# Expert biases of a mixture-of-experts kernel: gate's and up's selection products on two halves of TensorE's rows

## The reference

```python
counts = jnp.bincount(e_flat, length=N_EXPERTS)
padded = (counts + MOE_BLOCK - 1) // MOE_BLOCK * MOE_BLOCK
...
def expert_block(args):
    xb, e = args
    gu = xb @ w_gate_up[e] + b_gate_up[e]
    gate, up = jnp.split(gu, 2, axis=-1)
    gate = jnp.minimum(gate, SWIGLU_LIMIT)
    up = jnp.clip(up, -SWIGLU_LIMIT, SWIGLU_LIMIT)
    act = (up + 1.0) * gate * jax.nn.sigmoid(SWIGLU_ALPHA * gate)
    return act @ w_down[e] + b_down[e]
```

## Time and profile before

| | us |
|---|---|
| median of 3 runs | 2225.14 |
| lowest and highest | 2224.36, 2225.99 |
| profiled execution, its time | 2224.99 |
| its span in the trace | 2222.9 |
| TensorE busy | 2153.6 (97%) |
| VectorE busy | 1488.8 (67%) |
| ScalarE busy | 1075.6 (48%) |
| expert loop | some 1140, from 307 to about 1447 |

### The profile page before, as it was taken

The page is one execution under the profiler, slowest core; times in us unless marked ns, Lnnn a source line. Parts: engine busy times, 40 slices in busy tenths (PEclk is TensorE's granted clock), DMA queues, the critical chain, the costliest instruction groups (busy, mean ns, idle before and its releaser), DMA issues.

```text
span 2222.9 us, 26223 instructions
## 1 busy us (share of the span) xinstructions
PE 2153.6 (97%) x8888; PEld 1436.8 (65%) x8888; DVE 1488.8 (67%) x1474; ACT 1075.6 (48%) x1006; POOL 236.5 (11%) x239
## 2 busy tenths in 40 slices
PE   8999999999999999999999999959999999999998
PEld 3445447777777777777777777624654557888886
DVE  3953459999999999999999999843642323333333
ACT  1010147777777777777777777620003423222222
POOL 0003301211111121111112111100000000000000
PEclk9998989999999999999999999969999999999999
DMA  6123379999999999999999999822131011222220
GB/s 259 57 83 118 120 290 344 379 373 385 368 387 371 384 377 375 379 375 383 373 384 376 377 379 373 325 68 76 48 105 38 38 38 68 99 104 99 100 90 38
DMA packets 77757, 522.38 MB, mean 235 GB/s; under 512 B 10208, under 2 KB 10736, under 8 KB 21392
## 3 DMA queue, kind: packets, MB, share of 16 engines
q1 hardware_dynamic: 65088, 483.68, 56.0%
q0 software_dynamic: 9168, 31.01, 5.5%
q10 hardware_dynamic: 3456, 7.06, 1.0%
HBM read 500.72 MB, written 18.99 MB: 234 GB/s over the span
## 4 chain that ended last, share of the span: by engine, by line
PE 92%; DVE 5%; ACT 1%; DMA 1%; issue 0%; SPq 0%; DVEq 0%; ACTq 0%; POOLq 0%
PE bank L1021 21%; PE bank L1023 21%; PE bank L1022 21%; PE bank L887 8%; PE bank L1133 6%; DVE room L1338 3%; PE bank L1176 3%; PE bank L1234 2%; PE bank L1037 1%; PE bank L1148 1%; PE bank L993 1%; PE bank L1029 1%; PE bank L1206 1%; PE bank L1225 1%; PE bank L896 1%; PE bank L1188 1%
## 5 line engine op out<-in xcount | busy, mean ns | idle before, releaser
L1485 DVE TENSOR_TENSOR ring_r<-ring,room_r 128x2048 fp32r<-128x2048 f32 x384 | 873.5, 2289 | 89.6 <-ACT room_r L637 86.7
L637 ACT ACTIVATE room_r<-ring 128x2048 fp32r<-128x2048 f32 x384 | 735.5, 1916 | 189.1 <-PE bank L1023 183.4
L1021 PE MATMUL bank<-room_r 128*96 128x512 f32 x1536 | 606.7, 395 | 3.5 <-DVE room_r L1517 1.9
L1023 PE MATMUL bank<-room_r 128*96 128x512 f32 x1536 | 602.7, 392 | 0.0
L1022 PE MATMUL bank<-ring_r,room_r 128*96 128x512 f32 x1536 | 602.5, 392 | 0.0
L1021 PEld LDWEIGHTS bank<-room_r 128*96 128x96 f32 x1536 | 248.4, 162 | 105.9 <-DVE ring_r L1485 4.4
L1023 PEld LDWEIGHTS bank<-room_r 128*96 128x96 f32 x1536 | 248.2, 162 | 106.2
L1022 PEld LDWEIGHTS bank<-ring_r,room_r 128*96 128x96 f32 x1536 | 248.5, 162 | 101.4
L1133 PE MATMUL bank<-room,ring 128*128 128x512 f32 x320 | 140.4, 596 | 0.0
L1021 PE MATMUL bank<-room_r,ring_r 128*128 128x512 f32 x352 | 137.0, 389 | 0.9 <-DVE room_r L1736 0.9
L1023 PE MATMUL bank<-room_r,ring_r 128*128 128x512 f32 x352 | 136.9, 389 | 0.0
(11 more groups left out here) (249 smaller groups left out, 2189.5 us busy)
## 6 DMA issues: line engine op xcount, KB each, us to landing
ring<-in_wmoe SPq DMA_DIRECT2D x384, 1024.0 KB, 11.7
ring<-in_wf SPq DMA_DIRECT2D x33, 1024.0 KB, 4.8
ring<-in_wp SPq DMA_DIRECT2D x9, 2048.0 KB, 7.8
ring<-in_wd SPq DMA_DIRECT2D x7, 2048.0 KB, 8.6
ring<-in_wd SPq DMA_DIRECT2D x3, 1024.0 KB, 8.3
room<-in_xT SPq DMA_DIRECT2D x2, 1024.0 KB, 8.6
room<-in_xtok ACTq DMA_DIRECT2D x1, 2048.0 KB, 7.7
h_rows<-room POOLq DMA_DIRECT2D x4, 512.0 KB, 3.0
```

The source lines that it names most:

```text
L637: act.activation(w_hi[s_ % PAIRS], raw_w[ORDER[s_]], ACT.Copy)\
L1021: pe.matmul(out, x_hi, w_hi, start=start, stop=False, skip_group_check=True)
L1023: return pe.matmul(out, x_lo, w_hi, start=False, stop=stop, skip_group_check=True)
L1485: dve.tensor_tensor(w_lo[i], raw_w[i], w_hi[s_ % PAIRS].bitcast(F32), ALU.subtract)\
```

## The change

The host repeats the table four times over the partitions, so that 0 to 63 and 64 to 127 both carry it, and `expert` is p mod 32 everywhere. The addition of 1 covers all partitions; the subtraction is made twice, for partitions 32 to 63 and 96 to 127, and both waits for `bias_split` ask for 2. `biases` makes gate's product with rows 0 to 63 of the array and up's with rows 64 to 127. The order of the instructions on each engine stays; VectorE gets one more ahead of the loop.

```diff
             pool.wait_ge(s["bias_in"], 16)
-            up_bias = braw.rearrange("p (c h n) -> p c h n", c=CHUNKS, h=2)[0:2 * E, :, 1, :]
+            up_bias = braw.rearrange("p (c h n) -> p c h n", c=CHUNKS, h=2)[:, :, 1, :]
             pool.tensor_scalar(up_bias, up_bias, 1.0, None, ALU.add).then_inc(s["bias_one"], 1)
...
                 elif s_ == 0:
-                    act.wait_ge(s["bias_split"], 1)
+                    act.wait_ge(s["bias_split"], 2)
...
-            pe.wait_ge(s["bias_split"], 1)
+            pe.wait_ge(s["bias_split"], 2)
...
                 for h in range(2):
                     q = 2 * c + h
-                    pe.matmul(bank[q][0:CAP, :], sel_cur, bias_tab[:, q * 512:(q + 1) * 512], start=True, stop=False,
-                              skip_group_check=True)
+                    rows = slice(2 * E * h, 2 * E * (h + 1))
+                    pe.matmul(bank[q][0:CAP, :], sel_cur[rows, :], bias_tab[rows, q * 512:(q + 1) * 512], start=True,
+                              stop=False, skip_group_check=True)
...
             dve.wait_ge(s["bias_hi"], 1)
-            dve.tensor_tensor(bias_tab[E:2 * E, :], braw[E:2 * E, :], bias_tab[E:2 * E, :].bitcast(F32), ALU.subtract)\
-               .then_inc(s["bias_split"], 1)
+            for q in (E, 3 * E):
+                dve.tensor_tensor(bias_tab[q:q + E, :], braw[q:q + E, :], bias_tab[q:q + E, :].bitcast(F32), ALU.subtract)\
+                   .then_inc(s["bias_split"], 1)
...
-    c["expert"] = np.where(p < 2 * E, p % E, -1).astype(f)[:, None]
+    c["expert"] = (p % E).astype(f)[:, None]
...
-    bgu = np.zeros((P, 4 * 512), np.float32)
-    bgu[0:E] = bgu[E:2 * E] = x["b_gate_up"][0].reshape(E, 2, CHUNKS, 512).transpose(0, 2, 1, 3).reshape(E, -1)
-    arrays["bgu"] = bgu
+    arrays["bgu"] = np.tile(x["b_gate_up"][0].reshape(E, 2, CHUNKS, 512).transpose(0, 2, 1, 3).reshape(E, -1), (P // E, 1))
```

## The result

| | before | changed |
|---|---|---|
| median, 9 runs each | 2224.77 us | 2232.01 us |
| lowest and highest | 2223.96, 2226.31 | 2230.66, 2233.47 |
| profiled execution | 2224.99 us | 2231.58 us |
| its span | 2222.9 us | 2229.7 us |

The ratio is 1.0031, with a 95% interval of 1.0021 to 1.0042: 7.2 us more, inside the range of 2230 to 2248 and 3 us under the 2235 that was forecast.

The account below looks back on a forecast made before the run. TensorE's stream in the expert loop was taken as the bound. Profiled execution 2224.99 us + 9.6 for the bias pairs + 0 for the preparation = 2234.6, stated as 2235 us, range 2230 to 2248.

Parts of the forecast that it names:

- The bound: Expert loop: TensorE fully busy, 354.00 of 354 us, so time put into or taken out of its stream goes into the total.
- A passage at 0.17 us: Each change between 128 and 64 rows: 0.09 wait plus 0.08 unhidden load; two a pair, 0.34 us, 21.8 us over 64 pairs.
- The largest possible saving: Bias pairs in the loop: at most one 0.23 us step saved a pair, 64 x 0.23 = 14.7 us.
- The overlap: The two bias products of a pair partly run at once: net +0.15 us a pair, +9.6 us; chance 0.62.
- the right end: Lower end of the overlap case: both products of a pair start together, +0.11 us a pair, +7.0 us in all.
- The preparation at 0: Ahead of the loop: wider addition and second subtraction (2.28 us) absorbed in 7.60 us idle; cost 0, +2.3 if cover were gone.
- The signs: Expected in the trace after: bias load some 0.32 us behind L1023, L1023 to L1021 0.8 to 0.9 us, blocks up 0.3 us.
- One after another: Rival: the halves of a bias pair don't overlap in fp32r; +21.8 us, 2246.9; chance 0.22.
- Changes for free: Rival: loads at a change of rows hide behind running products, pairs keep their overlap; -14.7 us, 2210; chance 0.07.
- no effect: Rival: bias products on 64 rows run like those on 96 rows, without a gap; 2225 us; chance 0.05.
- More than the sum: Rival: an fp32r product's drain is longer, or the second subtraction loses its cover; up to 2250 and over; chance 0.04.
- The rule: Trainium skill, cited against the change: changing the tiling mode, not merely the tile, drains TensorE; earlier trace showed 0.09 us.

## Why the prediction came out as it did

- **The bound** was right. What an edit put into TensorE's stream of the loop or took out of it showed up in the total as often as the edit acts, from -4.3 to +44.2 us, and the only new waits are those of TensorE's own loads.
- **A passage at 0.17 us** was right and was the step on which all hung: 0.35 us for two, from scores in attention to fp32r products with 96 columns of weights. The largest possible saving, 14.7 us, was under this price of 21.8 us, so no degree of overlap could have made the change pay at this place.
- **The overlap** was the term that was mis-sized. I took the middle between both starting together (+0.11) and the second behind the first's load (+0.19), so +0.15 and 9.6 us. The loads of the two halves run at once (0.16 us for both), and the pair costs +0.12 in the middle and +0.11 at the start, where I had +0.15 for either: 7.2 us measured. My reading that a score's second load waits for its first was a row of one half, as the prediction itself said, and says nothing of two. The sentence of the Trainium skill (TensorE: Matmul & The Clock Gate, Measured speedup vs the span model) with its 4 ns for each further product gave the right end, +7.0. The trace of the changed kernel agrees: the two products of each of its 64 pairs start 3 to 4 ns apart.
- **The preparation at 0** was right, with the absorption in the idle time that was named.
- **The signs.** The load 0.32 us behind L1023 came as forecast, and the two products start together. One sign was wrong: from L1023 to L1021 I expected 0.8 to 0.9 us and it is 0.73 (535.44 to 536.17). The unhidden load of L1021 delays what stands behind it, L1022, and that is where the price has to be read. A block takes 0.23 us more, not 0.3.
- **The rivals.** One after another was priced at +21.8 and is what happens on the same half, +23.2. Changes for free and no effect are both excluded by the idle load at 535.76 and by the time. More than the sum didn't come about: the drain of an fp32r product is the same 0.09 us, and the subtraction kept its cover.
- **The rule.** That of the Trainium skill (TensorEngine Tiling, Key Properties) that a change of mode drains the engine and a change of tile does not agrees with all of it: no gap stands between the halves, and the earlier trace rows already had its 0.09 us.

## What to carry to other kernels

Products on halves of the array overlap fully, but the way in and the way out cost 0.35 us together here (96 columns of weights, 2.4 GHz level), 1.5 times what one 512-column product takes. Split such products only where at least two products are saved between one way in and one way out, and put them side by side in the program. With fewer moving columns each product saved should be worth less against the same price; no run here tried that. Before costing such a change, look in the trace for a place where the number of rows already falls to 64 or less, and read the distance of starts there.

## What was not expected of the hardware

TensorE starts products out of the order of the program when their halves of the array are free: L1041 at 553.37, before L1040 at 553.66. The time agrees, -3.0 us where strict order would have given +3.8. The Trainium skill says the opposite (TensorE: Matmul & The Clock Gate, The mechanism: products keep strict program order in their starts and ends, only weight loads are pulled ahead); the measurement decides, for starts at least. A semaphore signal on a later product may therefore not tell that an earlier one on the other half is done; no run here tried that, and the ends of products in the trace are modelled. And four products on quarters take as long as one, 0.47 us in the records.
